# A hybrid attention and MoE block: the first norm without root instructions, its tiles turned one by one, key and value weights loaded first

## The chip, the cores and the metric

The kernel runs on one core of a Trainium2 chip. The metric is device time in microseconds (us) of one execution. The core's engines run side by side, each through a list of its own, and meet at semaphores: PE (TensorE, matrix products and transposes), DVE (VectorE), ACT (ScalarE), POOL (GpSimd), and SP (SyncE), which here only issues DMAs.

## The reference, cut to what matters

One decoder block over 512 tokens of width 1024, float32:

```
h = x * rsqrt(mean(x*x) + 1e-6) * g1              # first norm
q, kc, vc, ks, vs, kw, vw, gates, ... = split(h @ w_in)
x = x + mixed(attention of two kinds, from those) @ w_out
x = x + moe(rms_norm(x), 32 experts, top 4)       # 12 MB of weights per expert
out = rms_norm(x)
```

Rope turns the keys ks and kw and the query by cos and sin of position times frequency. The change touches the first line, the rope angles and the weights of the second line's first products.

## The kernel before

Tokens lie on the partitions in four tiles of 128 (NT = 4), the width in eight chunks of 128 (NK = 8). All order is written by hand: each engine's program is one list, with semaphore waits between.

The start, which the change touches, goes so. SP (L485 to L496) issues the four tiles of x (512 KB each), then g1 (1024 single numbers of 4 bytes), f_bias, the rope frequencies twice, the positions, then `w_small`: the 792 columns of w_in for kc, vc, ks, vs, kw, vw and the NSA gates (3168 KB), and 8 columns for the decay (32 KB), then weights of the compression, of the gates and of the query. ACT squares each tile with a sum per token (L917) and, once DVE has made mean + eps of the sum (L1692), takes the root of it (L919). DVE then inverts the root, refines it in four small instructions (L1685 to L1688), and multiplies the tile by it (L1694). PE turns the tiles by transposes against the identity (L1191): chunk after chunk, and within the chunk tile after tile, so that eight PSUM banks fill one after the other:

```
for c in range(NK):
    for t in range(NT):
        if c == 0: pe.wait_ge(x_normed, t + 1)
        last = pe.transpose(...)
    last.then_inc(full, 1)
```

DVE meanwhile works out the rope angles in 16 instructions over 128x512 (L1699 to L1708), and only then copies the odd chunks out of PSUM times g1 (L1716). ACT waits for these angles too, takes sin and cos (L922, L923), and then copies the even chunks (L929). PE waits for the whole of `w_small` and for all eight copies (L1193 to L1195), and then starts the products (L1181): kc, vc, ks, kw, vs, vw in seven banks and then the gates. A product is 8 chunks; in float32 each chunk shows as two matmul instructions.

After kc and vc, ACT copies them out (L935, L936), then ks and kw (L941). POOL multiplies these by the cos (L726), PE swaps their halves (L1227) and DVE adds the sin part. From L1284 on come attention, the mixing products, the second norm (whose inverse root POOL takes as a power, L806), the router, and the 32 experts, whose weights stream through a ring of 12 buffers as PE frees them. POOL's own list begins with constants: identity, mask, `swap`, cmp_neg, cmp_one, kT_cmp, v_cmp and ones8 (L695 to L722).

Of the kernel before, what the change touches and what calls it, by code (L numbers as in the profile page):

```python
# [15 lines left out]
P = 128  # L16
# [127 lines left out]
def hybrid_block(nc, x, positions, norm1_g, w_in, cmp_pos_emb, cmp_w1, cmp_w2, fox_f_bias, w_proj_nsa,  # L144
                 w_proj_fox, w_out, norm2_g, router_w, router_b, expert_w1, expert_b1, expert_w2,
                 expert_b2, norm_f_g, rope_freqs, out):
    with ExitStack() as ctx:
# [121 lines left out]
        small_loaded = sem("small_loaded")  # L269
        pos_loaded = sem("pos_loaded")  # L270
        w_small_loaded = sem("w_small_loaded")
        w_cmp_loaded = sem("w_cmp_loaded")
# [210 lines left out]
        def _(sp):  # L483
            for t in range(NT):
                sp.dma_start(xs[:, t, :], x_v[:, t, :]).then_inc(rows_loaded[t], 16)  # L485
            sp.dma_start(g1[:, :], norm1_g[0].rearrange("(c p) -> p c", p=P), allow_slow_non_contiguous=True).then_inc(small_loaded, 16)
            sp.dma_start(f_bias[:, :], fox_f_bias[0:1, :].partition_broadcast(P)).then_inc(small_loaded, 16)
            for g in range(G):
                sp.dma_start(freq[DH * g:DH * (g + 1), :], rope_freqs[:, :]).then_inc(pos_loaded, 16)
            sp.dma_start(pos_i, positions[0:1, :].partition_broadcast(P)).then_inc(pos_loaded, 16)  # L490
            sp.dma_start(w_small[:, :, 0:C_FQ - C_KC], w_in_v[:, :, C_KC:C_FQ]).then_inc(w_small_loaded, 16)
            sp.dma_start(w_small[:, :, C_FQ - C_KC:], w_in_v[:, :, C_FF:C_GN]).then_inc(w_small_loaded, 16)
            for j in range(2):
# [192 lines left out]
        def _(pool):  # L686
            step = Steps(pool, pool_step)

            def take(semaphore, value):
# [6 lines left out]
            pool.affine_select(out=ident[:, :], in_=ident[:, :], compare_op=ALU.not_equal, fill=1.0, base=0,  # L696
                               pattern=[[-1, P]], channel_multiplier=1).then_inc(consts, 1)
            step.link(pool.memset(mask[:, :], 0.0))
            tri = mask[:, S - P:S]
# [4 lines left out]
            for g in range(G):  # L704
                lo, hi = (swap[:, DH * g + half * k:DH * g + half * (k + 1)] for k in range(2))
                step.link(pool.affine_select(out=lo, in_=lo, compare_op=ALU.not_equal, fill=-1.0,
                                             base=-half - DH * g, pattern=[[-1, half]], channel_multiplier=1))
                ins = pool.affine_select(out=hi, in_=hi, compare_op=ALU.not_equal, fill=1.0,
                                         base=-DH * g, pattern=[[-1, half]], channel_multiplier=1)
                if g:  # L710
                    ins.then_inc(consts, 1)
                else:
                    step.link(ins)
            step.link(pool.memset(cmp_neg[:, :, :, :], 0.0))
            step.link(pool.memset(cmp_one[:, :, :, :], 1.0))
# [187 lines left out]
        def _(act):  # L903
# [11 lines left out]
            for t in range(NT):  # L915
                act.wait_ge(rows_loaded[t], 16)
                act.activation(xn[:, t, :], xs[:, t, :], ACT.Square, accum_out=ss1[:, t:t + 1]).then_inc(squares, 1)  # L917
                act.wait_ge(mean_sq, t + 1)
                act.activation(tmp1[:, t:t + 1], ss1[:, t:t + 1], ACT.Sqrt).then_inc(root, 1)  # L919

            act.wait_ge(angles, 1)
            act.activation(rope_sin[:, :], ang[:, 0, :], ACT.Sin).then_inc(sines, 1)  # L922
            act.activation(rope_cos[:, :], ang[:, 1, :], ACT.Sin).then_inc(sines, 1)  # L923
            pre = PreFills()
            act.wait_ge(small_loaded, 32)
            for c in range(0, NK, 2):
# [3 lines left out]
            for k, name in enumerate(("kc", "vc")):  # L930
                b, n = pre(name)
                act.wait_ge(work_full[b], n + 1)
                for g in range(G):
                    src = work(b)[g * DH:(g + 1) * DH, :]
                    act.activation(kv_c[0:DH, k, g, :], src, ACT.Copy).then_inc(act_step, 1)  # L935
                    last = act.activation(kv_c[DH:P, k, g, 0:S - 1], src[:, 1:S], ACT.Copy)  # L936
                last.then_inc(work_free[b], 1)
            for name, dst in (("ks", q_plain), ("kw", q_rope)):
                b, n = pre(name)
                act.wait_ge(work_full[b], n + 1)  # L940
                act.activation(dst, work(b), ACT.Copy).then_inc(work_free[b], 1)  # L941
                act.wait_ge(work_free[b], n + 1)
                act.sem_inc(raw_k_ready, 1)
# [227 lines left out]
        def _(pe):  # L1171
# [13 lines left out]
            pe.wait_ge(consts, 1)  # L1185
            for c in range(NK):
                w, full = bank(pre, "hT%d" % c)
                for t in range(NT):
                    if c == 0:
                        pe.wait_ge(x_normed, t + 1)  # L1190
                    last = pe.transpose(w[:, t * P:(t + 1) * P], xn[:, t, c * P:(c + 1) * P], ident[:, :])  # L1191
                last.then_inc(full, 1)
            pe.wait_ge(w_small_loaded, 32)  # L1193
            for b in range(NK):
                pe.wait_ge(work_free[b], 1)  # L1195

            def small(at, n):
                return lambda c: w_small[:, c, at - C_KC:at - C_KC + n]

            for name, at in (("kc", C_KC), ("vc", C_VC), ("ks", C_KS), ("kw", C_KW)):  # L1200
                w, full = bank(pre, name)
                matmuls(w, small(at, P), lambda c: hT[:, c, :], NK).then_inc(full, 1)
            for name, src, n, tiles in (("vs", small(C_VS, P), P, range(NT)), ("vw0", small(C_VW, N_VW), N_VW, (0, 1)),
# [464 lines left out]
        def _(dve):  # L1668
# [11 lines left out]
            def inverse_root(ss, r, t1, t2, count):  # L1680
# [7 lines left out]
                step.link(dve.tensor_tensor(r, r, t2, ALU.mult))  # L1688

            for t in range(NT):  # L1690
                dve.wait_ge(squares, t + 1)
                step.link(mean_square(ss1[:, t:t + 1], ss1[:, t:t + 1], EPS))  # L1692
                inverse_root(ss1[:, t:t + 1], rs1[:, t:t + 1], tmp1[:, t:t + 1], tmp2[:, t:t + 1], t + 1)
                dve.tensor_scalar(xn[:, t, :], xs[:, t, :], rs1[:, t:t + 1], None, ALU.mult).then_inc(x_normed, 1)  # L1694


            dve.wait_ge(pos_loaded, 48)
            turns_, a0, posf = ang[:, 2, :], ang[:, 3, :], ang[:, 3, :]
# [10 lines left out]
            dve.sem_inc(angles, 1)  # L1709

            dve.wait_ge(small_loaded, 32)
            pre = PreFills()
            for c in range(1, NK, 2):
                b, n = pre("hT%d" % c)
                dve.wait_ge(work_full[b], n + 1)
                dve.tensor_scalar(hT[:, c, :], work(b), g1[:, c:c + 1], None, ALU.mult).then_inc(work_free[b], 1)  # L1716


# [233 lines left out]
            def refined(t):  # L1952
                one = slice(t, t + 1)
                dve.wait_ge(power, t + 1)
                step.link(dve.scalar_tensor_tensor(tmp4[:, one], tmp3[:, one], ss2[:, one], tmp3[:, one], ALU.mult, ALU.mult))
# [239 lines left out]
            def finished(t):  # L2195
                dve.wait_ge(squares, 3 * NT + t + 1)
                step.link(mean_square(ss2[:, t:t + 1], ss2[:, t:t + 1], EPS))
                inverse_root(ss2[:, t:t + 1], rs2[:, t:t + 1], tmp3[:, t:t + 1], tmp4[:, t:t + 1], NT + t + 1)
                dve.scalar_tensor_tensor(y_in[t][:, 1, :], y_in[t][:, 0, :], rs2[:, t:t + 1], gf_b, ALU.mult, ALU.mult)\
                    .then_inc(result, 1)  # L2200

            dve.wait_ge(pos_loaded, 64)
            for t in range(NT):
# [24 lines left out]
```

## Time and profile before

| | us |
|---|---|
| median of 3 runs (lowest, highest) | 1676.53 (1675.32, 1678.14) |
| the profiled execution | 1675.77 |
| its span in the trace | 1674.0 |
| PE busy | 1591.8, 95% of the span |
| DVE, ACT, POOL busy | 440.9, 259.8, 233.9 |

The span runs from the first to the last instruction of the trace; 1.8 us of the execution's own time lie outside it. Busy shares are means over stages of different limits. Durations of PE's instructions are modelled, since they overlap in its pipeline: the distance between two starts is what one costs. Starts and durations are in us, "mean" and min/median/max of instructions in ns.

### The profile page before, as it was taken

Reading aid. Unit: us, or ns where it says so; the run is one execution under the profiler, and the core shown is the slowest. Engines: PE = TensorE matmul, PEld = TensorE weight load, DVE = VectorE, ACT = ScalarE, POOL = GpSimd, SP = SyncE. Lnnn points to the kernel's source line nnn. Section 1 sums busy time; section 2 is a strip of 40 time slices with the busy share of each in tenths; the row PEclk is TensorE's granted clock in tenths of the full one; section 3 lists DMA queues with packets and bytes.
Section 4 is the critical chain, followed back from the end, with each engine's and each line's share of the span. In section 5 each row is a group of like instructions: output and inputs, shape, how many; then the busy total and the mean of one; then the engine's idle time right before and its main releaser. Section 6 shows DMA issues by size and latency. Waiting matters only on the chain.

```text
span 1674.0 us, 32752 instructions
## 1 busy us (share of the span) xinstructions
PE 1591.8 (95%) x13380; PEld 645.9 (39%) x13381; DVE 440.9 (26%) x966; ACT 259.8 (16%) x541; POOL 233.9 (14%) x377
## 2 busy tenths in 40 slices
PE   5999999999999789999999999999999999999992
PEld 2654555565445323333333333333333333333331
DVE  4012555332325422113111311131112111211222
ACT  3212444323322100000000000000000000000002
POOL 1000000522200101111111111111111111121101
PEclk8999999999999799999999999999999999999996
DMA  8023120431251789999999999999999999999995
GB/s 224 1 54 73 38 76 13 136 88 51 65 200 51 275 342 376 388 393 386 396 386 395 392 399 386 391 394 399 389 396 399 401 389 394 400 402 390 400 383 177
DMA packets 150302, 472.35 MB, mean 282 GB/s; under 512 B 30537, under 2 KB 71497, under 8 KB 117458
## 3 DMA queue, kind: packets, MB, share of 16 engines
q1 hardware_dynamic: 137458, 446.56, 69.1%
q0 software_dynamic: 12800, 25.17, 6.9%
q8 instruction: 31, 0.51, 0.1%
q14 instruction: 13, 0.11, 0.0%
HBM read 452.41 MB, written 19.29 MB: 282 GB/s over the span
## 4 chain that ended last, share of the span: by engine, by line
PE 88%; DVE 5%; ACT 3%; issue 2%; DMA 1%; DVEq 0%; PEld 0%; POOL 0%; ACTq 0%; PEldq 0%; POOLq 0%; SPq 0%
PE ps L1562 40%; PE ps L1580 13%; PE ps L1181 12%; PE ps L1584 7%; PE ps L1510 3%; PE ps L1323 3%; PE ps L1308 2%; PE ps L1595 2%; PE ps L1536 2%; ACT mixT L995 2%; PE ps L1285 1%; ACT mixT L1004 1%; PE ps L1295 1%; DVE ps L1797 1%; PE ps L1556 1%
## 5 line engine op out<-in xcount | busy, mean ns | idle before, releaser
L1562 PE MATMUL ps<-ring,oT_fox 128*32 128x512 f32 x6144 | 668.8, 595 | 0.0
L1562 PEld LDWEIGHTS ps<-ring,oT_fox 128*32 128x32 f32 x6144 | 184.1, 110 | 462.8 <-issue 459.2
L1580 PE MATMUL ps<-ring,hT 128*32 128x512 f32 x2048 | 264.1, 592 | 0.0
L2101 DVE TENSOR_TENSOR mixT<-ps,mask 128x768 f32<-128x768 f32 x64 | 61.1, 954 | 650.2 <-PE ps L1562 650.2
L1584 PE MATMUL ps<-ring,hT 128*32 128x256 f32 x2048 | 154.8, 379 | 0.0
L1323 PE MATMUL ps<-hT,ring 128*128 128x512 f32 x304 | 137.3, 599 | 0.0
L1584 PEld LDWEIGHTS ps<-ring,hT 128*32 128x32 f32 x2048 | 61.3, 110 | 158.4 <-issue 158.4
L1119 ACT ACTIVATE mixT<-mixT 128x768 f32<-128x768 f32 x32 | 27.0, 845 | 609.8 <-DVE mixT L2105 609.8
L1181 PE MATMUL ps<-hT,ring 128*128 128x512 f32 x208 | 93.2, 609 | 7.0 <-ACT hT L929 7.0
L841 POOL COPY pT<-pT 96x32 bf16 (+1 forms) x64 | 13.8, 218 | 575.5 <-ACT hT L1129 566.3
L2130 DVE COPY hT<-ps 128x384 f32<-128x384 f32 x64 | 32.8, 553 | 181.0 <-PE ps L1595 180.9
L1323 PEld LDWEIGHTS ps<-hT,ring 128*128 128x128 f32 x304 | 55.5, 191 | 64.2 <-issue 64.2
L1129 ACT ACTIVATE hT<-ps,v_fox 128x512 f32<-128x512 f32 x64 | 33.7, 577 | 295.9 <-PE ps L1584 295.9
L1580 PEld LDWEIGHTS ps<-ring,hT 128*32 128x32 f32 x2048 | 61.1, 110 | 46.5
L1181 PEld LDWEIGHTS ps<-hT,ring 128*128 128x128 f32 x208 | 40.2, 195 | 56.5 <-issue 56.4
L995 ACT ACTIVATE mixT<-ps,st 128x128 f32<-128x128 f32 (+1 forms) x96 | 49.1, 536 | 78.1 <-DVE st L1803 78.1
L1510 PE MATMUL ps<-ring,mixT 128*128 128x512 f32 x128 | 59.0, 601 | 2.1 <-DVE qk L1930 2.1
L832 POOL DMA_INDIRECT x<-hT,v_win x32 | 50.6, 1580 | 26.2 <-POOL v_win L829 24.5
L834 POOL DMA_INDIRECT x<-hT,v_win x32 | 49.7, 1552 | 9.8 <-issue 9.8
L1181 PEld LDWEIGHTS ps<-ring,hT 128*128 128x128 f32 x384 | 45.2, 192 | 2.3 <-issue 2.3
L1181 PE MATMUL ps<-ring,hT 128*128 128x128 f32 (+1 forms) x384 | 45.5, 279 | 0.0
L818 POOL COPY v_win<-v_win 96x1 int32 (+1 forms) x30 | 5.9, 196 | 259.4 <-DMA x<-hT,v_win 231.0
(291 smaller groups left out, 1162.4 us busy)
## 6 DMA issues: line engine op xcount, KB each, us to landing
ring<-in_expert_w SPq DMA_DIRECT2D x384, 1024.0 KB, 19.8
ring<-in_w_in SPq DMA_DIRECT2D x28, 512.0 KB, 4.8
ring<-in_w_out SPq DMA_DIRECT2D x8, 512.0 KB, 7.6
ring<-in_w_in SPq DMA_DIRECT2D x1, 3168.0 KB, 12.9
xs<-in_x SPq DMA_DIRECT2D x4, 512.0 KB, 5.1
ring<-in_w_in SPq DMA_DIRECT2D x8, 256.0 KB, 3.6
ring<-in_w_proj_nsa SPq DMA_DIRECT2D x16, 128.0 KB, 2.9
ring<-in_w_proj_fox SPq DMA_DIRECT2D x8, 256.0 KB, 3.3
```

The source lines that it names most:

```text
L832: pool.indirect_dma_start(out=x2_half, out_offset=bass.IndirectOffsetOnAxis(ap=now_half[b], axis=0), in_=yb[b][:, 0:512], in_offset=None, ...
L834: pool.indirect_dma_start(out=x2_quarter, out_offset=bass.IndirectOffsetOnAxis(ap=now_quarter[b], axis=0), in_=yb[b][:, 512:768], in_offse ...
L995: last = act.activation(probs[:, h, P_OFF[t]:P_OFF[t] + P * (t + 1)], scores(h, t), ACT.Exp, bias=ngm[:, h, t:t + 1], accum_out=sums[:, h, ...
L1129: ins = act.activation(yb[b][:, cols], y_ps[:, cols], ACT.Copy, scale=gate)
L1181: last = pe.matmul(dst, lhs(c), rhs(c), start=(c == 0), stop=(c == n - 1))
L1308: ins = pe.matmul(o_bank[h * DH:(h + 1) * DH, kt * P:S], v[:, kt, h * DH:(h + 1) * DH], pT[:, h, at:at + S - kt * P], start=(first and n = ...
L1323: ins = pe.matmul(w, w_c(c), hT[:, c, :], start=(c == 0), stop=(c == NK - 1))
L1510: ins = pe.matmul(ps[:, u, :], mixT[:, k, t * P:(t + 1) * P], w_o[k][:, n * 512:(n + 1) * 512], start=(k == 0), stop=(k == NK - 1))
L1562: ins = pe.matmul(wide(ps[TG * j:TG * j + TG, g, :]), xT[b][:, c, TG * g:TG * g + TG], up_slab(c, j), start=(c == 0), stop=(c == NK - 1), ...
L1580: pe.matmul(ps[TG * q:TG * q + TG, 4, :], gT[b][:, 2 * (q // 2) + h, TG * j:TG * j + TG], ring[:, NK + j, at:at + 512], start=False, stop= ...
L1584: ins = pe.matmul(ps[TG * q:TG * q + TG, 5, 0:256], gT[b][:, 4 + h, TG * j:TG * j + TG], ring[:, NK + j, at:at + 256], start=False, stop=( ...
L2101: return dve.tensor_tensor(to, half, b_up[:, 256 * n:256 * n + 256].unsqueeze(1).broadcast_to([P, NG, 256]), ALU.add)
```

## The change

- ACT takes the four squares one after the other; its four roots go. POOL raises each mean to the power -0.5 (in between its constants, after `swap`), against a constant -0.5 that it writes into `hbias` first. DVE refines the power in three small instructions instead of a reciprocal and four, and makes the mean of the next tile before it refines this one.
- PE turns tile after tile, all eight chunks of a tile as soon as it is normed. The first product waits for each copied chunk as it comes to it, instead of for all eight ahead.
- DVE copies the odd chunks ahead of the angles. ACT copies the even chunks ahead of sin and cos, which it takes between its copies of kc and of vc.
- SP: the kc and vc columns (256 of the 792, 1024 KB) are loaded right behind x, ahead of g1, with a semaphore of their own. The other 536 columns (2144 KB) and the 8 of the decay come next, then f_bias, frequencies and positions, which come ahead of `w_small` in the kernel before.

```
@@ sync
             for t in range(NT):
                 sp.dma_start(xs[:, t, :], x_v[:, t, :]).then_inc(rows_loaded[t], 16)
+            sp.dma_start(w_small[:, :, 0:2 * P], w_in_v[:, :, C_KC:C_KC + 2 * P]).then_inc(w_kv_loaded, 16)
             sp.dma_start(g1[:, :], norm1_g[0].rearrange("(c p) -> p c", p=P), allow_slow_non_contiguous=True).then_inc(small_loaded, 16)
-            sp.dma_start(f_bias[:, :], fox_f_bias[0:1, :].partition_broadcast(P)).then_inc(small_loaded, 16)
+            sp.dma_start(w_small[:, :, 2 * P:C_FQ - C_KC], w_in_v[:, :, C_KC + 2 * P:C_FQ]).then_inc(w_small_loaded, 16)
+            sp.dma_start(w_small[:, :, C_FQ - C_KC:], w_in_v[:, :, C_FF:C_GN]).then_inc(w_small_loaded, 16)
+            sp.dma_start(f_bias[:, :], fox_f_bias[0:1, :].partition_broadcast(P)).then_inc(pos_loaded, 16)
             for g in range(G):
                 sp.dma_start(freq[DH * g:DH * (g + 1), :], rope_freqs[:, :]).then_inc(pos_loaded, 16)
             sp.dma_start(pos_i, positions[0:1, :].partition_broadcast(P)).then_inc(pos_loaded, 16)
-            sp.dma_start(w_small[:, :, 0:C_FQ - C_KC], w_in_v[:, :, C_KC:C_FQ]).then_inc(w_small_loaded, 16)
-            sp.dma_start(w_small[:, :, C_FQ - C_KC:], w_in_v[:, :, C_FF:C_GN]).then_inc(w_small_loaded, 16)
@@ gpsimd, after the identity; and after swap
+            step.link(pool.memset(hbias[:, :], -0.5))
...
+            for t in range(NT):
+                pool.wait_ge(mean_sq, t + 1)
+                pool.tensor_tensor(tmp1[:, t:t + 1], ss1[:, t:t + 1], hbias[:, :], ALU.pow).then_inc(power, 1)
@@ scalar
                 act.activation(xn[:, t, :], xs[:, t, :], ACT.Square, accum_out=ss1[:, t:t + 1]).then_inc(squares, 1)
-                act.wait_ge(mean_sq, t + 1)
-                act.activation(tmp1[:, t:t + 1], ss1[:, t:t + 1], ACT.Sqrt).then_inc(root, 1)
-            act.wait_ge(angles, 1)
-            act.activation(rope_sin[:, :], ang[:, 0, :], ACT.Sin).then_inc(sines, 1)
-            act.activation(rope_cos[:, :], ang[:, 1, :], ACT.Sin).then_inc(sines, 1)
...
                 last.then_inc(work_free[b], 1)
+                if k == 0:
+                    act.wait_ge(angles, 1)
+                    act.activation(rope_sin[:, :], ang[:, 0, :], ACT.Sin).then_inc(sines, 1)
+                    act.activation(rope_cos[:, :], ang[:, 1, :], ACT.Sin).then_inc(sines, 1)
@@ tensor
-            for c in range(NK):
-                w, full = bank(pre, "hT%d" % c)
-                for t in range(NT):
-                    if c == 0:
-                        pe.wait_ge(x_normed, t + 1)
+            for t in range(NT):
+                pe.wait_ge(x_normed, t + 1)
+                for c in range(NK):
+                    w, full = bank(pre, "hT%d" % c)
                     last = pe.transpose(w[:, t * P:(t + 1) * P], xn[:, t, c * P:(c + 1) * P], ident[:, :])
-                last.then_inc(full, 1)
-            pe.wait_ge(w_small_loaded, 32)
-            for b in range(NK):
-                pe.wait_ge(work_free[b], 1)
+                    if t == NT - 1:
+                        last.then_inc(full, 1)
+            def first_hT(c):
+                pe.wait_ge(work_free[c], 1)
+                return hT[:, c, :]
+            pe.wait_ge(w_kv_loaded, 16)
             for name, at in (("kc", C_KC), ("vc", C_VC), ("ks", C_KS), ("kw", C_KW)):
+                if name == "ks":
+                    pe.wait_ge(w_small_loaded, 32)
                 w, full = bank(pre, name)
-                matmuls(w, small(at, P), lambda c: hT[:, c, :], NK).then_inc(full, 1)
+                matmuls(w, small(at, P), first_hT if name == "kc" else lambda c: hT[:, c, :], NK).then_inc(full, 1)
@@ vector
+            first_mean(0)
             for t in range(NT):
-                dve.wait_ge(squares, t + 1)
-                step.link(mean_square(ss1[:, t:t + 1], ss1[:, t:t + 1], EPS))
-                inverse_root(ss1[:, t:t + 1], rs1[:, t:t + 1], tmp1[:, t:t + 1], tmp2[:, t:t + 1], t + 1)
-                dve.tensor_scalar(xn[:, t, :], xs[:, t, :], rs1[:, t:t + 1], None, ALU.mult).then_inc(x_normed, 1)
-            dve.wait_ge(pos_loaded, 48)
+                if t < NT - 1:
+                    first_mean(t + 1)
+                ss, r, t2, rs = (v[:, t:t + 1] for v in (ss1, tmp1, tmp2, rs1))
+                dve.wait_ge(power, t + 1)
+                step.link(dve.scalar_tensor_tensor(t2, r, ss, r, ALU.mult, ALU.mult))
+                step.link(dve.tensor_scalar(t2, t2, -0.5, 1.5, ALU.mult, ALU.add))
+                step.link(dve.tensor_tensor(rs, r, t2, ALU.mult))
+                dve.tensor_scalar(xn[:, t, :], xs[:, t, :], rs, None, ALU.mult).then_inc(x_normed, 1)
+            dve.wait_ge(small_loaded, 16)
+            (the four copies of the odd chunks, L1713 to L1716)
+            dve.wait_ge(pos_loaded, 64)
             (the angles, L1698 to L1709)
```

The counts of `power`, `root` and `pos_loaded` that later stages wait for are moved by the same numbers.

## Rows read from the trace of the kernel before

**Rows 1.** The page, first part: busy us, share of the span, instructions.
```profile
PE 1591.8 (95%) x13380; PEld 645.9 (39%) x13381; DVE 440.9 (26%) x966; ACT 259.8 (16%) x541; POOL 233.9 (14%) x377
```
**Rows 2.** What PE waited for, 0 to 150 us: total, times, longest.
```profile
PE ps L1191 <- DVE mixT L1694: 13.6, 4, 8.8
PE ps L1181 <- ACT hT L929: 7.0, 1, 7.0
```
**Rows 3.** The chain of waits, 0 to 150 us: start, length, what.
```profile
0.84 3.35 DMA xs<-in_x
...
23.45 0.44 DVE oT_nsa L1708
...
25.11 2.32 ACT hT L929 x4
27.78 60.12 PE ps L1181 x224
```
**Rows 4.** Windows: busy (x) of PE, PEld, DVE, ACT, POOL, granted clock, DMA share, GB/s.
```profile
27.80:33.00 5.20, 5.20 (x6) 2.13 (x7) 0.00 (x0) 0.00 (x0) 0.00 (x0) 0.50 1.08 252
33.00:34.00 1.00, 1.00 (x3) 0.53 (x2) 0.00 (x0) 0.00 (x0) 0.00 (x0) 0.74 1.35 218
...
548.00:576.00 28.00, 18.37 (x166) 10.76 (x168) 18.27 (x58) 4.35 (x7) 5.26 (x9) 0.63 0.77 270
```
**Rows 5.** Line L1181, the products, in 34:37 us.
```profile
L1181 PE MATMUL ps<-hT,ring x8: 592/592/593, 33.7 to 36.7; 128*128 128x512 f32 x8
```
**Rows 6.** Line L1191, the transposes, in 17:19 and 20.1:20.8 us: ns min/median/max, starts.
```profile
L1191 PE MATMUL ps<-ident,mixT x11: 421/421/421, 16.8 to 18.9; 128*128 128x128 f32 x11
...
L1191 PE MATMUL ps<-ident,mixT x6: 272/273/273, 19.9 to 20.5; 128*128 128x128 f32 x6
```
**Rows 7.** Timeline of PE, 10 to 180 us.
```profile
15.02 5.72 PE L1191 MATMUL ps<-ident,mixT 128*128 128x128 f32 x29 [1.64 <-DVE mixT L1694]
...
87.74 1.88 PE L1227 MATMUL ps<-qk,swap 128*128 128x512 f32 x4
```
**Rows 8.** Timeline of ACT, 0 to 30 us: start, length, instruction [idle before].
```profile
4.21 1.06 ACT L917 ACTIVATE mixT<-xs 128x1024 f32<-128x1024 f32 x1 [2.09 <-DMA xs<-in_x]
...
5.38 1.28 ACT L919 ACT_TABLE_LOAD   x1
```
**Rows 9.** Timeline of DVE, 0 to 30 us.
```profile
5.39 0.15 DVE L1678 TENSOR_SCALAR st<-st 128x1 f32<-128x1 f32 x1 [5.28 <-ACT mixT L917]
...
7.68 0.16 DVE L1688 TENSOR_TENSOR st<-st 128x1 f32<-128x1 f32 x1
7.88 0.75 DVE L1694 TENSOR_SCALAR mixT<-xs,st 128x1024 f32<-128x1024 f32 x1
...
14.88 0.42 DVE L1699 CAST oT_nsa<-oT_fox 128x512 f32<-128x512 int32 x1
...
24.10 2.73 DVE L1716 TENSOR_SCALAR hT<-ps,g 128x512 f32<-128x512 f32 x4 [0.23 <-DVE oT_nsa L1708]
```
**Rows 10.** Line L485 (loads of x): issue starts, then landing.
```profile
L485 SPq DMA_DIRECT2D xs<-in_x x4: 381/426/432, 0.8 to 2.2; - x4
...
DMA to landing us min/median/max: 3.3/5.1/6.9
```
**Rows 11.** Line L806, POOL's power in the second norm: ns min/median/max.
```profile
L806 POOL TENSOR_TENSOR v_win<-v_win,kT_win x4: 549/554/578, 496.5 to 550.9; 128x1 f32<-128x1 f32 x4
```
**Rows 12.** Timeline of SP's issues, 0 to 200 us.
```profile
2.69 0.47 SPq L486 DMA_DIRECT2D g<-in_norm_g  x1
...
7.24 3.08 SPq L492 DMA_DIRECT2D ring<-in_w_in  x1
```
**Rows 13.** DMA issues, 0 to 60 us: KB each, us from issue to landing.
```profile
ring<-in_w_in SPq DMA_DIRECT2D x1, 3168.0 KB, 12.9
...
ring<-in_w_in SPq DMA_DIRECT2D x1, 32.0 KB, 14.7
...
g<-in_norm_g SPq DMA_DIRECT2D x1, 4.0 KB, 5.9
```

More of the change, by code:

```diff
@@ L270, in hybrid_block @@
         pos_loaded = sem("pos_loaded")
+        w_kv_loaded = sem("w_kv_loaded")
         w_small_loaded = sem("w_small_loaded")
@@ L917, in _ @@
                 act.activation(xn[:, t, :], xs[:, t, :], ACT.Square, accum_out=ss1[:, t:t + 1]).then_inc(squares, 1)
-                act.wait_ge(mean_sq, t + 1)
-                act.activation(tmp1[:, t:t + 1], ss1[:, t:t + 1], ACT.Sqrt).then_inc(root, 1)
-            act.wait_ge(angles, 1)
-            act.activation(rope_sin[:, :], ang[:, 0, :], ACT.Sin).then_inc(sines, 1)
-            act.activation(rope_cos[:, :], ang[:, 1, :], ACT.Sin).then_inc(sines, 1)
             pre = PreFills()
-            act.wait_ge(small_loaded, 32)
+            act.wait_ge(small_loaded, 16)
             for c in range(0, NK, 2):
@@ L1688, in inverse_root, with first_mean @@
                 step.link(dve.tensor_tensor(r, r, t2, ALU.mult))
+            def first_mean(t):
+                dve.wait_ge(squares, t + 1)
+                mean_square(ss1[:, t:t + 1], ss1[:, t:t + 1], EPS).then_inc(mean_sq, 1)
+            first_mean(0)
             for t in range(NT):
-                dve.wait_ge(squares, t + 1)
-                step.link(mean_square(ss1[:, t:t + 1], ss1[:, t:t + 1], EPS))
-                inverse_root(ss1[:, t:t + 1], rs1[:, t:t + 1], tmp1[:, t:t + 1], tmp2[:, t:t + 1], t + 1)
-                dve.tensor_scalar(xn[:, t, :], xs[:, t, :], rs1[:, t:t + 1], None, ALU.mult).then_inc(x_normed, 1)
-            dve.wait_ge(pos_loaded, 48)
+                if t < NT - 1:
[7 more added lines that the diff above has]
+            dve.wait_ge(small_loaded, 16)
+            pre = PreFills()
+            for c in range(1, NK, 2):
+                b, n = pre("hT%d" % c)
+                dve.wait_ge(work_full[b], n + 1)
+                dve.tensor_scalar(hT[:, c, :], work(b), g1[:, c:c + 1], None, ALU.mult).then_inc(work_free[b], 1)
+            dve.wait_ge(pos_loaded, 64)
             turns_, a0, posf = ang[:, 2, :], ang[:, 3, :], ang[:, 3, :]
@@ L1709, in _ @@
             dve.sem_inc(angles, 1)
[L1711 to L1716, printed above, removed]
             for k in range(2):
@@ L1953, in refined @@
                 one = slice(t, t + 1)
-                dve.wait_ge(power, t + 1)
+                dve.wait_ge(power, NT + t + 1)
                 step.link(dve.scalar_tensor_tensor(tmp4[:, one], tmp3[:, one], ss2[:, one], tmp3[:, one], ALU.mult, ALU.mult))
@@ L2197, in finished @@
                 step.link(mean_square(ss2[:, t:t + 1], ss2[:, t:t + 1], EPS))
-                inverse_root(ss2[:, t:t + 1], rs2[:, t:t + 1], tmp3[:, t:t + 1], tmp4[:, t:t + 1], NT + t + 1)
+                inverse_root(ss2[:, t:t + 1], rs2[:, t:t + 1], tmp3[:, t:t + 1], tmp4[:, t:t + 1], t + 1)
                 dve.scalar_tensor_tensor(y_in[t][:, 1, :], y_in[t][:, 0, :], rs2[:, t:t + 1], gf_b, ALU.mult, ALU.mult)\
                     .then_inc(result, 1)
-            dve.wait_ge(pos_loaded, 64)
+            dve.wait_ge(pos_loaded, 80)
             for t in range(NT):
```

## The prediction, written before the changed kernel ran

> **What bounds the kernel now.** I read the busy shares first: PE works 95% of the span [rows 1], so only what keeps PE idle, or slow while busy, is to be had. Next, PE's waits in the first 150 us [rows 2]: 13.6 us for normed tiles and 7.0 us for copied chunks; these two are what it waits for ahead of the products. The chain of waits [rows 3] says what makes them: the load of x, the norm, then the rope angles on DVE (the last ends at 23.9), then ACT's even copies (25.11 + 2.32 = 27.4), and from 27.78 on PE without a break for 60 us. So the angles, which no product of that stretch needs, stand between the transposes and the products. What begins at 27.78 is the work of the whole kernel: each us by which it begins earlier is a us of the total, as long as no later wait is tied to something that does not move with it.
>
> The second thing to see is PE's pace. The products begin at half clock: 6 in 5.2 us at a granted 0.50, which is 1.2 GHz, and 0.74 in the next us, so the rise to 2.4 GHz came at about 33.5 [rows 4]. After it one costs (36.7 - 33.7) / 7 = 0.43 us [rows 5]. Half clock therefore cost (33.5 - 27.8) / 2 = 2.9 us. The transposes tell of the clock too: 10 starts in 16.8 to 18.9, so 0.21 each, and 421 ns of duration; later 272 ns and (20.5 - 19.9) / 5 = 0.12 each [rows 6]. So the clock rose there too, at about 19.9, some 4.9 us after PE's busy stretch began at 15.02 [rows 7].
>
> **The change part by part.** I rebuild the start in its new order, in trace time.
>
> *Squares.* The first square starts at 4.21 and DVE sees its sum at 5.39 [rows 8, 9], so a square holds ACT for about 1.2 us. The root, its table load of 1.28 and the wait for DVE's mean leave ACT's list [rows 8]. Then the loads count: x is issued at 0.8 to 2.2 and lands after 3.3 to 6.9 us, the last at 2.2 + 6.9 = 9.1 [rows 10]. The last square thus starts at about 9.4 (behind a third that lands in between) and its sum is there at 10.6; the third's at 9.4.
>
> *Power and refinement.* POOL's power is not in this place before; in the second norm it takes 0.55 [rows 11]. I take 0.65 with its semaphore, from 0.55 to 1.2 (twice). Before it, a mean is 0.2; behind it, three small instructions at 0.2 each and the multiplication of 0.75 [rows 9]: 1.35 of DVE for a tile. It makes the next mean ahead of that, so tile 0 ends at about 8.05 (5.39 + 0.2, second mean at 6.7, + 1.35), tile 1 waits for the third sum: 9.6 + 1.35 = 10.95; mean 3 at 11.15; tile 2 ends at 12.5, tile 3 at 13.85. The power runs beside this. The wait puts POOL's later constants (L714 to L722) behind the last power, at about 11.9; their first user on DVE comes after L1227 at 87.7 [rows 7]. Cost nothing; with the cover gone, each us of POOL would be one of PE.
>
> *Transposes.* 8 per tile: 8 x 0.213 = 1.7 us at half clock, 8 x 0.12 = 0.95 at full. At half: tile 0 in 8.2 to 9.9, tile 1 in 11.0 to 12.7, then without idle time 14.4 and 16.1. At full for the last tile alone 13.9 to 14.9. The first product needs these and the first copy: four on DVE take 2.73, so 0.7 each [rows 9], started when chunk 0 is full (13.95 to 14.6). Copies and transposes overlap; later chunks come every 0.35 us from two engines, and a chunk's two product instructions take 0.86: PE never waits for them. First product between 15.0 and 16.2; I take 15.8. Gain 27.8 - 15.8 = 12.0.
>
> *The clock.* Before, it rose 4.9 us after PE became busy in the transposes [rows 6, 7] and 5.7 after in the products [rows 4]. It was down again by the products because PE idled from 20.8 [rows 7] to 27.8. Now PE is busy from 11.0 with no such idle time behind. I take a rise at 16.3: a loss of 0.25 in place of 2.9, gain 2.6; between 0 (the loss stays 2.9) and 2.9.
>
> Here a page of the Trainium skill speaks against this term: "TensorE: Matmul & The Clock Gate", Part 4, PE-mode transpose, holds that transposes do not count as activity that brings the full clock. By this the products would start cold. The rows disagree, since transposes sped up from 421 to 272 ns with nothing but transposes running; I keep it as a rival.
>
> *Loads.* The kc and vc columns are 1024 KB behind 2048 KB of x. The old single load moved 3168 KB in 12.9 us [rows 13], 4.1 us per 1024 KB, so at worst they land 4.2 us behind x, at 13.3; with the rate of x itself (2048 KB by 9.1, from 0.84) at about 12. Either is before 15.8. g1 is issued about 0.5 later than at 2.69 [rows 12] and lands 5.9 after issue [rows 13]: 9.1, plus 2.6 to 4.2 for the 1024 KB now ahead of it: 11.7 to 13.3, against the 14 at which the first copy wants it. This has the smallest margin of all. If its 4-byte pieces mix with the 2144 KB behind them (8.7 us at that rate) it lands as late as 22. The other 2144 KB are wanted by ks, 32 products of 0.43 behind 15.8: 29.5. The decay columns, the last of the old order, landed at 7.24 + 14.7 = 21.9 [rows 12, 13] with the same bytes ahead. f_bias, frequencies and positions come behind them: by 24 at the latest. SP's issues of compression, gate and query weights keep their order and the bytes ahead of them.
>
> *Angles and sines.* 23.9 - 14.9 = 9.0 us of DVE, from 17 (copies done) or from 24: done at 26 to 33. ACT takes sin and cos between kc's and vc's copies, and holds vc, ks and kw behind them. PE first needs them for the swaps, at 87.7 [rows 7], which 14.6 earlier is 73.1: behind ACT's copies of vc, ks and kw and POOL's products with the cos there are 40 us of cover. Cost nothing; past it, 1 us for 1 us.
>
> *Sum.* 12.0 + 2.6 = 14.6 us. All later waits are for work or for buffers that move with PE, so I let it pass to the end. One thing can shift: the granted clock drops again in later pauses (0.63 in 548 to 576, [rows 4]), and where its rise falls within them can move by a us or two either way.
>
> Of the profiled execution, 1675.8 - 14.6 = 1661.2; the median of before lies 0.7 above that execution, so 1661.9 as a median. Two executions of before differ by up to 2.8 us, so about 0.2% (3.4 us) is what can be told from no change.
>
> **The rivals.**
> - *As summed.* 1661.9; its own range is 1658 (first product at 14.5 and full clock, 16.2 saved, and 2 for the later clock) to 1664. Chance 0.62.
> - *Transposes in pieces leave the clock down.* For: PE idles about 1.1 us between tiles 0 and 1. Against: [rows 6]. Products start at 16.2 and run 5.7 us at half: gain 11.6, time 1664.9 as a median. Chance 0.17. The page of the Trainium skill named above gives the same time.
> - *g1 or the kc and vc columns are late.* For: g1 is 1024 pieces of 4 bytes, now behind 1024 KB. First product at 19 to 22.5, the pause brings half clock back: gain 5.3 to 8.8, time 1667.5 to 1671. Chance 0.14.
> - *The gain is given back* (a weight load of the experts that does not move earlier, or the clock in a later pause): within 3.4 us of before, about 1675. Chance 0.03.
> - *Slower: the second load of `w_small` decides.* PE waits at ks for both the 2144 KB and the decay columns, which are 1024 pieces of 32 bytes. It costs 1 us for each us behind 29.5 at which they land, and makes the kernel slower only from 44 on; [rows 12, 13] have them at 21.9. At 50 the time would be 1682. Chance 0.03, with the same wait at ACT for angles past 60 in it.
> - *The change doesn't do what it says.* The copies and the products might still wait for all of `w_small`; the code shows none, and it would give 22, as in the case of g1. Chance 0.01.
>
> **How the numbers follow.** The likeliest is 1661.9. Low end 1657.5, the best of the first case less half the spread; high end 1669.5, into the late loads, with about 0.12 left above and 0.04 below. Faster by over 0.2%: 0.62 + 0.17 + 0.14 + 0.01 = 0.94; same 0.03; slower 0.03.
>
> **What would show it.** The chain from x to the first product with L1181 at 14.5 to 16.2; no angle in that chain; PE's wait for copies near nothing; transposes in four groups; products at 0.43 from the start or within 1 us; POOL's first power near 5.6 and 0.55 long; sin and cos between 26 and 33. Wrong: a first product past 18, a half-clock stretch of over 3 us in the products, PE waiting before ks, or a distance between first product and end that has grown by over 3 us.

## The result, and the profile after

| | before | after |
|---|---|---|
| median, us | 1676.6 | 1661.1 |
| lowest to highest | 1675.3 to 1678.1 | 1660.4 to 1661.4 |
| profiled execution (span) | 1675.8 (1674.0) | 1660.9 (1659.2) |

The ratio is 0.9906, with a 95% interval of 0.9895 to 0.9918: 15.5 us, faster, clear of the noise. The forecast was 1661.9, in a range of 1657.5 to 1669.5. Measured twice more (e1, e11 below), the same changed kernel took 1660.9 and 1661.9 us beside 1676.8 and 1675.9 for before.

What PE waited for in the first 150 us of the changed kernel (engine, line, releaser: total us, times, longest), to be held against [rows 2]:

```profile
PE ps L1195 <- DVE mixT L1713: 8.5, 2, 8.3
...
PE ps L1186 <- ACT hT L930: 0.2, 1, 0.2
```

The wait for the copied chunks was 7.0 us and is 0.2. Of the 8.5 us for normed tiles 8.3 are the wait ahead of the first tile. The chain of waits over the same stretch (start, length, what), against [rows 3]:

```profile
1.75 5.57 DMA xs<-in_x
7.33 1.16 ACT mixT L923 x2
...
12.00 0.88 DVE mixT L1713
12.93 0.34 PE ps L1195
13.36 0.70 ACT hT L930
14.19 57.28 PE ps L1186 x224
...
93.17 15.63 PE ps L1186 x32
```

No angle is left in it. The first product starts at 14.19 where it started at 27.78, and the 224 instructions that follow take 57.28 us where they took 60.12: that is 13.6 and 2.8 us, together 16.4 us ahead. The last row is read further down.

DVE and POOL, from their timelines, against [rows 9, 11]. DVE makes the first mean at 5.44, as before (5.39); the fourth tile's multiplication starts at 12.00 in place of 14.21:

```profile
5.44 0.15 DVE L1688 TENSOR_SCALAR st<-st 128x1 f32<-128x1 f32 x1 [5.32 <-ACT mixT L923]
...
12.00 0.87 DVE L1713 TENSOR_SCALAR mixT<-xs,st 128x1024 f32<-128x1024 f32 x1
13.49 2.72 DVE L1720 TENSOR_SCALAR hT<-ps,g 128x512 f32<-128x512 f32 x4 [0.61 <-PE ps L1195]
20.23 0.43 DVE L1724 CAST oT_nsa<-oT_fox 128x512 f32<-128x512 int32 x1 [4.02 <-DMA oT_fox<-in_positions]
```

```profile
5.67 0.58 POOL L719 TENSOR_TENSOR st<-st,hbias 128x1 f32<-128x1 f32 x1 [1.52 <-DVE st L1688]
...
10.98 0.74 POOL L721 MEMSET cmp_one<- 128x256 f32 x1
```

The angles start when the positions land, at 20.2; sin follows at 29.3. The loads (KB each, us from issue to landing), against [rows 13]:

```profile
ring<-in_w_in SPq DMA_DIRECT2D x1, 2144.0 KB, 12.9
...
ring<-in_w_in SPq DMA_DIRECT2D x1, 1024.0 KB, 8.6
...
g<-in_norm_g SPq DMA_DIRECT2D x1, 4.0 KB, 8.5
```

Issued at 2.69, 3.24 and 4.36, these three landed at 11.3 (kc and vc columns), 11.7 (g1) and 17.3 (the rest). The first copy starts at 13.36, on ACT, so g1 had 1.6 us to spare.

The clock. Transposes (line L1195) in 9.4:11 and in 11:12.5 us, and the first products (L1186) in 14:17, ns min/median/max, then starts:

```profile
L1195 PE MATMUL ps<-ident,mixT x8: 421/421/468, 9.4 to 10.9; 128*128 128x128 f32 x8
L1195 PE MATMUL ps<-ident,mixT x13: 272/273/421, 10.7 to 12.5; 128*128 128x128 f32 x13
```

```profile
L1186 PE MATMUL ps<-hT,ring x7: 593/593/667, 14.2 to 16.8; 128*128 128x512 f32 x7
```

As in [rows 6], 421 ns is a transpose at half clock and 272 one at full; their distances, 0.21 and 0.11 us, halve as well. The short ones begin at 11.7, and the first clock record of the trace, full, stands at 11.65. So the rise came there, while PE had run nothing but transposes, and every product, from the first, ran at full clock. In e1 and e11 the same rise came at 13.3 and 13.6. The windows can't show it, since they count the time ahead of the first record as full clock. Here is 8 to 11 us, with transposes of 421 ns (busy of PE, PEld, DVE, ACT, POOL, then clock, DMA share, GB/s):

```profile
8.00:11.00 3.00, 2.70 (x13) 2.54 (x14) 2.43 (x11) 1.63 (x4) 1.38 (x4) 1.00 1.13 332
```

### The profile page after: what moved, and what is told of

It reads as the page before. It is cut to its first block, busy times and chain, and to the rows that moved or that the text cites. A ratio compares the mean times of both kernels' runs of the same rounds, so it can differ in the third digit from the quotient of the medians.

```text
span 1659.2 us, 32738 instructions
## 1 busy us (share of the span) xinstructions
PE 1589.3 (96%) x13380; PEld 645.0 (39%) x13381; DVE 438.8 (26%) x958; ACT 258.1 (16%) x536; POOL 237.3 (14%) x382
## 4 chain that ended last, share of the span: by engine, by line
PE 89%; DVE 4%; ACT 3%; issue 2%; DMA 1%; DVEq 0%; PEld 0%; POOL 0%; SPq 0%; ACTq 0%; PEldq 0%; POOLq 0%
PE ps L1572 40%; PE ps L1590 13%; PE ps L1186 12%; PE ps L1594 7%; PE ps L1520 4%; PE ps L1333 3%; PE ps L1318 2%; ACT mixT L1000 2%; PE ps L1605 2%; PE ps L1546 2%; PE ps L1295 1%; ACT mixT L1009 1%; PE ps L1305 1%; PE ps L1566 1%; DVE ps L1814 1%
## 5 line engine op out<-in xcount | busy, mean ns | idle before, releaser
L847 POOL COPY pT<-pT 96x32 bf16 (+1 forms) x64 | 13.7, 216 | 574.6 <-ACT hT L1134 565.4
L1186 PE MATMUL ps<-hT,ring 128*128 128x512 f32 x208 | 92.1, 603 | 0.2 <-ACT hT L930 0.2
L1186 PEld LDWEIGHTS ps<-hT,ring 128*128 128x128 f32 x208 | 39.7, 193 | 49.0 <-issue 48.8
L1186 PEld LDWEIGHTS ps<-ring,hT 128*128 128x128 f32 x384 | 45.2, 192 | 2.3 <-issue 2.3
L1186 PE MATMUL ps<-ring,hT 128*128 128x128 f32 (+1 forms) x384 | 45.5, 279 | 0.0
## 6 DMA issues: line engine op xcount, KB each, us to landing
ring<-in_w_in SPq DMA_DIRECT2D x1, 2144.0 KB, 12.9
```

The costliest lines, as they stand in the source:

```text
L1186: last = pe.matmul(dst, lhs(c), rhs(c), start=(c == 0), stop=(c == n - 1))
```

## The experiments

All times are medians. e1 to e4, e5 to e8, e9 to e11, and e12 are four groups, each measured beside its own runs of the kernel before, whose medians were 1676.8, 1676.3, 1675.9 and 1677.2; the ratios are to these. "Rest" is the time from the swaps after ks and kw (L1227 before) to the end of the span: what lies behind the stretch that the change touches. Starts are in us of each run's one trace.

| | median, us | ratio to before (95%) | first product | swaps | rest |
|---|---|---|---|---|---|
| before | 1676.6 | | 27.8 | 87.7 | 1586.3 |
| changed | 1661.1 | 0.9906 (0.9895, 0.9918) | 14.2 | 71.3 | 1587.9 |
| e1 again | 1660.9 | 0.9905 (0.989, 0.992) | 14.8 | 71.9 | 1587.5 |
| e2 old loads | 1669.6 | 0.9956 (0.9941, 0.9971) | 20.8 | 79.5 | 1588.2 |
| e3 angles first | 1679.6 | 1.0016 (1.0007, 1.0026) | 31.2 | 91.3 | 1586.3 |
| e4 split | 1661.9 | 0.9911 (0.9897, 0.9924) | 15.1 | 72.2 | 1587.3 |
| e5 roots back | 1664.1 | 0.9921 (0.9907, 0.9935) | 16.7 | 73.8 | 1588.8 |
| e6 by chunk | 1664.1 | 0.9932 (0.9919, 0.9946) | 18.5 | 75.5 | 1586.8 |
| e7 all copies | 1664.4 | 0.9925 (0.9912, 0.9939) | 17.8 | 76.6 | 1587.4 |
| e8 copies only | 1669.2 | 0.9951 (0.9938, 0.9965) | 21.2 | 78.3 | 1590.2 |
| e9 last norm | 1664.4 | 0.9934 (0.992, 0.9947) | 15.6 | 72.7 | 1590.0 |
| e10 third on ACT | 1665.1 | 0.9938 (0.9925, 0.9952) | 14.5 | 71.6 | 1592.1 |
| e11 again | 1661.9 | 0.9922 (0.9908, 0.9935) | 15.0 | 72.2 | 1588.0 |
| e12 third only | 1662.1 | 0.9909 (0.9892, 0.9925) | 14.0 | 71.2 | 1587.6 |

### e1 and e11: the changed kernel again

No edit.

> The changed kernel itself, once more. In its trace the first product starts 13.6 us earlier and all products run at full clock (another 2.9), so PE is 16.4 us ahead at the swaps (87.9 against 71.5); but the span is only 14.8 shorter. 1.7 is lost at 93 to 97, right behind the small products of the compression, where the granted clock is 0.50, and 1.7 more at 464 to 468; before has neither of these dips. Theory: the time of the start is fixed, and the dips are not part of the change: they fall in or out with where PE's thin stretches lie in time, so a second execution shows the first product within 0.3 us of 14.2, and either dip may be missing (a span 1.7 shorter) or there. Rival: the dips are made by the new schedule and stand in every execution at the same places; then this trace shows both, and the median is 1661.1 again with a spread under 1 us.

> The changed kernel a third time, beside e9 and e10. Theory (half-clock stretches fall in and out, the start is fixed up to the landing of x): first product at 14.2 to 15.2, the time from the swaps to the end 1587 to 1588, median 1661 within 1. Rival: a trace with both dips again at 93 and 464, as in the first.

The chain of e1 (start, length, what), and granted clock in windows of the first trace of the changed kernel (busy of PE, PEld, DVE, ACT, POOL, then clock, DMA share, GB/s):

```profile
14.82 57.28 PE ps L1186 x224
...
93.84 13.93 PE ps L1186 x32
```

```profile
92.00:96.00 4.00, 4.00 (x37) 2.37 (x35) 1.51 (x8) 0.26 (x1) 0.00 (x0) 0.70 0.07 15
96.00:100.00 4.00, 4.00 (x9) 1.67 (x8) 0.00 (x0) 0.00 (x0) 0.00 (x0) 0.88 0.00 0
```

In the first trace the 32 products behind the compression took 15.63 us, 1.7 more than the 13.93 in e1 and e11: a half-clock stretch lies at 93.6 to 97.0, and e1 and e11 have none there. The stretch at 466 is in the first and in e11 (464), missing in e1, and e1 has one at 286 to 290 that the first has not. The theory holds as far as that they come and go between executions of one program while the median stays; what makes one fall in is not shown. The first product came at 14.2, 14.8 and 15.0: e1's 0.3 bound was too tight, since the last of x lands at 8.5 to 9.1 and the clock rose at 11.7, 13.3 and 13.6, within the transposes.

### e2: the old loads

```
-            sp.dma_start(w_small[:, :, 0:2 * P], w_in_v[:, :, C_KC:C_KC + 2 * P]).then_inc(w_kv_loaded, 16)
...
             sp.dma_start(pos_i, positions[0:1, :].partition_broadcast(P)).then_inc(pos_loaded, 16)
+            sp.dma_start(w_small[:, :, 0:C_FQ - C_KC], w_in_v[:, :, C_KC:C_FQ]).then_inc(w_small_loaded, 16)
+            sp.dma_start(w_small[:, :, C_FQ - C_KC:], w_in_v[:, :, C_FF:C_GN]).then_inc(w_small_loaded, 16)
...
-            pe.wait_ge(w_kv_loaded, 16)
+            pe.wait_ge(w_small_loaded, 32)
```

> The changed kernel with the loads of the kernel before: x, g1, f_bias, frequencies, positions, the 792 columns in one piece, the 8 decay columns; the first product waits for all of them. Theory (the split load is what lets products start at 14.2): they landed at 21.9 before, so the first product starts at about 22, 7.8 later, after a pause of PE of 8 us, and begins at half clock for some 5 us (2.9 lost): 10 to 11 us slower than the changed kernel, about 1671.5. Rival (the columns are there anyway, the order of the loads buys little because x and g1 are what is waited for): under 3 us slower, below 1664.

The chain:

```profile
7.54 13.25 DMA ring<-in_w_in
20.84 58.84 PE ps L1184 x224
```

The first product starts at 20.8, released by the decay columns, after a pause of PE of 5.8 us. The products take 58.84 instead of 57.28, so 1.6 us are lost to half clock. The median is 8.7 us above e1's (the traces' starts give 6.0 and 1.6): the theory, under its 10 to 11, since the columns landed 1.1 us earlier than it had them, e1 itself started 0.6 later than the first trace that the sum was made from, and half clock cost 1.6 and not 2.9.

### e3: the angles first again

On DVE the 16 instructions of the angles stand ahead of the four copies again, and on ACT:

```
+            act.wait_ge(angles, 1)
+            act.activation(rope_sin[:, :], ang[:, 0, :], ACT.Sin).then_inc(sines, 1)
+            act.activation(rope_cos[:, :], ang[:, 1, :], ACT.Sin).then_inc(sines, 1)
             pre = PreFills()
             act.wait_ge(small_loaded, 16)
```

> The changed kernel with the rope angles on DVE and sin and cos on ACT ahead of the copies again, all else as changed, the positions behind the weights in the load order too. Theory: the angles cannot start before the positions land (20.2 in the changed kernel's trace), take 9 us, and then come sin, cos and the copies: first product at 31 to 33, half clock for over 5 us: 17 to 19 + 2.9 = 20 to 22 us slower than the changed kernel, 1681 to 1683, so slower than the kernel before. Rival (the angles are short of the weights anyway, so their place is worth only what lies behind 22): first product near 27, about 1677.

The chain:

```profile
15.47 4.78 DMA oT_fox<-in_positions
...
29.89 0.61 ACT rope_cos L927
30.51 0.58 ACT hT L933
31.23 60.24 PE ps L1185 x224
```

As the theory had it: first product at 31.2, at half clock, 18.7 us above e1, and a kernel that is no faster than before, and by its interval 0.07% to 0.26% slower, though norm, loads and transposes are all changed. The new load order puts the positions at 20.2, and is good only together with the new place of the angles.

### e5, e6, e7: one part undone each

In e5 ACT's roots, DVE's reciprocal and its four instructions are back and POOL's powers gone:

```
+                act.wait_ge(mean_sq, t + 1)
+                act.activation(tmp1[:, t:t + 1], ss1[:, t:t + 1], ACT.Sqrt).then_inc(root, 1)
```

In e6 the two loops of the transposes are exchanged again, in e7 the single wait is back:

```
-            for t in range(NT):
-                pe.wait_ge(x_normed, t + 1)
-                for c in range(NK):
+            for c in range(NK):
+                for t in range(NT):
```

```
+            for b in range(NK):
+                pe.wait_ge(work_free[b], 1)
```

> The changed kernel with ACT's roots and DVE's reciprocal and four refinement instructions again in the first norm; POOL's powers gone. Theory (the roots held ACT's next square and set the pace of a tile to 2.1 us, as in the kernel before): the last tile is normed near 15.0 instead of 12.9, the first product starts at 16.2 to 16.5 instead of 14.2 to 14.8 in the two traces of the changed kernel: 1.5 to 2.2 us slower. Rival (x lands at 8.6 only and sets the pace, so the roots were hidden): under 0.7 us.

> The changed kernel with transposes chunk by chunk again, so that 29 of 32 wait for the last normed tile at 12.9. Theory (PE and its clock): 29 transposes, first at 0.21 us and the last few at 0.12 as in the kernel before, end at about 18.5; first product at 18.6 to 19, at full clock; 4 to 5 us slower. Rival (the copies are what the first product waits for, and turning early is worth only the 1.7 us by which 8 transposes at half clock exceed 1): under 2.5 us.

> The changed kernel with one wait for all eight copied chunks ahead of the first product. Theory: the last copy ends at 16.2, so the first product starts at 16.3 instead of 14.2; the pause of 2.4 us leaves the clock full: 1.7 to 2.3 us slower. Rival (the pause brings half clock back): 2.9 more, 5 us slower.

The first product's row of the chain in e5, e6 and e7, then e7's wait and its clock (same columns as above):

```profile
16.68 57.28 PE ps L1184 x224
```

```profile
18.62 57.04 PE ps L1186 x224
```

```profile
17.82 58.97 PE ps L1186 x224
```

```profile
PE ps L1186 <- DVE hT L1718: 2.4, 1, 2.4
```

```profile
17.80:24.00 6.20, 6.18 (x11) 2.70 (x12) 3.44 (x7) 0.00 (x0) 0.00 (x0) 0.72 0.86 164
```

e5: the first product starts 1.6 to 2.5 us later than in the three traces of the changed kernel; from the last landing of x on it is 1.2 to 1.9 later. That is the theory, in its trace. e6: 3.4 to 4.3 later (its first product starts at 18.46, just before the last transpose ends), at full clock; a little under the theory. In e7 the first product starts at 17.8 in place of the foretold 16.3, since the last of x landed at 9.1 and the clock rose only at 14.8, so that the transposes ended later. And a second point was foretold wrong: behind the pause of 2.4 us the clock fell, at 18.2, and the products took 1.7 us more. This is its one trace, of an execution of 1665.8 us; the others took 1662.3 to 1666.6, and whether each of them had the fallen clock is not shown.

The medians say less. No changed kernel was measured in this group; against before the three gain 12.2, 12.3 and 11.9 us, the changed kernel 15.9, 14.0 and 15.5 in its groups. So each part is worth about 2 to 4 us, and the interval of each ratio overlaps with that of e11.

### e8: the copies alone, on the kernel before

DVE's four copies stand ahead of its angles, and on ACT:

```
-            act.wait_ge(angles, 1)
-            act.activation(rope_sin[:, :], ang[:, 0, :], ACT.Sin).then_inc(sines, 1)
-            act.activation(rope_cos[:, :], ang[:, 1, :], ACT.Sin).then_inc(sines, 1)
...
+                if k == 0:
+                    act.wait_ge(angles, 1)
...
```

> The kernel before with one part of the change alone: the copies ahead of the angles on DVE, and ahead of sin and cos on ACT, which takes these between kc and vc. Loads, roots, transposes and the two waits of the first product as before. Theory: transposes end at 20.8, the decay columns land at 21.9, the copies end by 22.3, so the first product starts near 22.3 in place of 27.8, after a pause of PE of 1.5 us only, at full clock: gain 5.5 + 2.9 = 8.4 us over the kernel before, about 1668.3. Rival (clock not kept): the first product starts at 22.3 at half clock, gain 5.5, 1671.2.

PE's wait and the chain:

```profile
PE ps L1182 <- DMA ring<-in_w_in: 1.0, 1, 1.0
```

```profile
21.16 57.28 PE ps L1182 x224
```

A pause of 1.0 us left the clock full: theory. The median is 7.2 us below before's, not the 8.4 foretold: at the swaps the trace is 9.4 us ahead, and its rest is 3.9 longer than before's, with half-clock stretches at 100 and 472 that before has not, beside one at 141 that stands for before's at 150, and a longer one from 544 on.

This one reordering of two engines' lists is about half of the whole gain; the load order is the other half only once it is there. A comparison with e2 shows the same for the rest: e2 has the roots, the tile-wise transposes and the wait chunk by chunk as well, but the old loads, and its first product starts at 20.8 against 21.2 here. Its transposes end at 15.0 in place of 20.1, and PE then waits 5.8 us for the columns and loses its full clock. Without the new load order these three parts bring nothing: 1669.6 against 1669.2, or 7.1 and 7.2 us of gain over before.

### e4: full products between the thin ones

```
+            pe.wait_ge(w_gate_loaded[0], 64)
+            project_gate(pre, "gn2", 0, 0)
             for l in range(CB // 2):
                 for k in range(2):
                     last = pe.matmul(w[DH * k:DH * (k + 1), n:n + 1], w_c1[:, k, l, :], pos_c[:, k, l:l + 1],
...
-            project_gates(2)
+            project_gate(pre, "gf2", 0, 1)
```

> The changed kernel with one of the two gate products of the third gate pair (gn2, 6.9 us of full products) moved between the two loops of small products of the compression (64 of 62 columns, 64 of one column, 5.6 us together). Theory: the clock fell at 93 because these 5.6 us use little of the array; with full products between them no half-clock stretch follows, and the median is 1.0 to 1.7 us lower, 1659.4 to 1660, if the dip stands in most executions of the changed kernel. Rival (the dip is chance, or comes from elsewhere): within 0.5 us of the changed kernel, or a half-clock stretch is still seen at 90 to 105.

The chain of e4:

```profile
88.27 3.61 PE ps L1254 x60
91.89 7.06 PE ps L1186 x16
98.95 1.96 PE ps L1260 x64
100.91 0.34 PE ps L1266 x4
101.25 8.76 PE ps L1186 x16
```

The half-clock stretch is there all the same, behind the second loop (8.76 us against 7.06), and the median is 1.0 us above the changed kernel's. My remedy failed. Of the 14 traces here, six have a stretch behind the compression (changed, e2, e4, e8, e10, e12). That thin products cause it is not shown, only that it stands behind them when it comes.

### e9: the last norm treated alike

```
-                act.wait_ge(mean_sq, 2 * NT + t + 1)
-                act.activation(tmp3[:, t:t + 1], ss2[:, t:t + 1], ACT.Sqrt).then_inc(root, 1)
+                pool.wait_ge(mean_sq, 2 * NT + t + 1)
+                pool.tensor_tensor(tmp3[:, t:t + 1], ss2[:, t:t + 1], minus_half, ALU.pow).then_inc(power, 1)
```

> The changed kernel with the same treatment of the last norm, which ends the program: no roots on ACT, POOL's power of each mean against its constant -0.5, three refinement instructions on DVE, the next mean ahead of the multiplication. Theory (this norm is on the path to the end, one tile's DVE work after the other): in the kernel before a tile takes 2.65 us (starts of its last DVE instruction 1661.76, 1664.40, 1667.05, 1669.69) and the first is ready for it 2.4 after its mean, with a table load of 1.28 in that. With powers a tile takes 2.05 (0.15 + 0.6 + 1.29) and the first 1.5: 0.9 + 3 x 0.6 = 2.7 us faster than the changed kernel, 1658.3. Rival (the loads of the rows and the stores behind set this end): under 0.8 us.

POOL at the end of e9, and DVE's first two tiles:

```profile
1649.64 0.57 POOL L909 TENSOR_TENSOR v_win<-v_win,kT_win 128x1 f32<-128x1 f32 x1 [13.72 <-issue]
1651.12 1.51 POOL L909 TENSOR_TENSOR v_win<-v_win,kT_win 128x1 f32<-128x1 f32 x1 [0.91 <-DVE v_win L1689]
```

```profile
1644.14 0.15 DVE L1689 TENSOR_SCALAR v_win<-v_win 128x1 f32<-128x1 f32 x1 [24.89 <-ACT ring L1174]
...
1650.24 0.22 DVE L2222 SCALAR_TENSOR_TENSOR v_win<-v_win 128x1 f32<-128x1 f32 x1 [5.95 <-POOL v_win L909]
...
1652.67 0.22 DVE L2222 SCALAR_TENSOR_TENSOR v_win<-v_win 128x1 f32<-128x1 f32 x1 [0.44 <-POOL v_win L909]
```

2.5 us slower than e11 beside it, where 2.7 faster was expected. The mean is there at 1644.3, but POOL takes it up at 1649.6. The 13.7 us ahead of that are no rest: POOL's list waits until 1639.4 for its last scatter to land, and from 1640.2 to 1649.5 it goes through the loop over extra expert blocks, 21 times with nothing to do, 0.44 us each. Its sequencer's rows show the loop:

```profile
L889 POOLq ALU_OP  x21: 32/32/38, 1640.6 to 1649.4; - x21
```

In the kernel before and in the changed one nothing comes behind this loop on POOL, so its length does not matter there. And a power that meets DVE's multiplication takes 1.51 in place of 0.57. A tile takes 2.43 in place of 2.65, which wins back 0.7. From the first mean to the end of the span e9 takes 18.6 us, the changed kernel 14.7.

### e10 and e12: the third tile multiplied by ACT

```
+            act.activation(xn[:, 2, :], xs[:, 2, :], ACT.Copy, scale=rs1[:, 2:3]).then_inc(third_normed, 1)
```

> e9 with, in the first norm, the multiplication of the third tile on ACT instead of DVE, so that DVE refines the fourth meanwhile. Theory: the fourth tile is normed 0.7 us earlier and the first product starts that much earlier, if x lands as before: 0.5 to 0.7 us faster than e9, which only its trace can tell (the distance from the last landing of x to the first product: 14.19 - 8.6 = 5.6 in the changed kernel, 5.0 here). Rival (turning the third tile is what holds the fourth): the distance stays 5.6.

> The changed kernel with the third tile of the first norm multiplied on ACT, the last norm as before. In e10 the last tile of x landed at 9.2 and the first product started at 14.5, 5.3 later; in four traces with DVE alone it took 5.6 to 6.3 (5.6 in the changed kernel, 6.3 in e1, 5.9 in e11, 6.3 in e9). Theory: 5.0 to 5.4 here, so the median is 0.5 to 1 us under the changed kernel's 1661.1: 1660.3. Rival (the clock's half stretches, 1.7 us each, cover a gain of this size): a median anywhere in 1659.5 to 1662.5, not told from the changed kernel.

e10 is on e9, e12 on the changed kernel. From the last landing of x to the first product: 5.3 and 5.5 us, against 5.6, 6.3, 5.9 in the changed kernel's three traces and 6.3 in e9. But the distance hangs on the clock too, which rose in the transposes at 11.7, 13.3 and 13.6 in the changed kernel's traces, at 15.1 in e9, 12.2 in e10 and 11.8 in e12. e12 and the first trace, alike in this, differ by nothing (5.54 against 5.57). And in e12 PE waits for a normed tile once only, ahead of the first:

```profile
PE ps L1202 <- DVE mixT L1724: 8.7, 1, 8.7
```

From 8.7 on it turns tiles without a break, so what holds the first product is the turning, as e10's rival had it. An earlier fourth tile can be worth little: PE waits 0.2 us for it in the first trace and not at all in e1 and e11. The medians (1665.1 beside 1664.4; 1662.1) show no gain either. No version measured here beats the changed kernel.

## Why the prediction was right

The total was met within 0.8 us, but with some luck: the start gained 1.8 us more than summed, and 1.6 us of the lead were lost behind it, which the sum did not have.

- *What bounds.* Right: the angles ahead of the copies and the loads behind them held the products. e3 shows the one (18.7 us above e1), e2 the other (8.7).
- *First product at 15.8, gain 12.0.* It came at 14.2, gain 13.6, just outside the 14.5 to 16.2 that I gave as the sign; at 14.8 and 15.0 in e1 and e11. The tiles were ready at 12.9 in place of 13.85, since the third of x landed at 7.3 and the last at 8.6, not 9.1; and from 11.7 on the transposes ran at full clock. The sign "transposes in four groups" did not come: tiles 0 to 2 are turned in one go, with one short wait ahead of tile 3.
- *The clock, 2.6.* It was 2.8: [rows 3] have 60.12 for the 224 instructions, after has 57.28. The clock came up with nothing but transposes running, at 11.7 in place of 16.3; at 13.3 and 13.6 in e1 and e11, still ahead of the products. "TensorE: Matmul & The Clock Gate" in the Trainium skill (Part 4, PE-mode transpose) says that the full clock does not engage for them. The rows above decide against it for the float32 transposes of this kernel, and the rival that it stood beside, 1664.9, fell.
- *Power, POOL's constants, sines: nothing.* Right. A power took 0.55 to 0.58 us in the first norm. POOL's constants ended at 14.1, sin and cos came at 29.3 to 30.4, and PE came to the swaps without a wait.
- *g1 late.* It landed at 11.7, the early end of my 11.7 to 13.3. The kc and vc columns landed at 11.3, 2.7 behind x. My "about 12" for them did not follow from the rate that I gave for it, which is the same 4.1 us per 1024 KB as the other; it is the spacing of x's landings (1.3 to 1.8 us per 512 KB) that holds here.
- *All of it passes to the end.* Not quite: 16.4 us ahead at the swaps, 14.8 in the span. The difference of 1.6 is a balance of half-clock stretches. The first trace has short ones at 94, 135 and 466, before's has one at 150, each worth about 1.7 us, so those at 135 and 150 cancel; [rows 4] show a later one that both have, and it is 20.5 us long in before, 17.1 here. Matched instruction by instruction, the lead is 14.8 us behind the first stretch (DVE's copy at 123.89 and 109.08), 13.2 behind the third (486.35 and 473.17), 14.1 behind the later one (591.59 and 577.48) and 14.8 at the last norm (1659.36 and 1644.57). The stretch at 94 also lies in products and is over the 3 us that I named as a sign of being wrong; in the first 224 products, which that term was about, there is none. e1 and e11 show the stretches moving between executions. With one trace of before I can't say whether before has fewer of them in the mean: over the medians of three groups the gain is 15.5, 15.9 and 14.0, where the swaps of their traces give 15.6 to 16.4.

Taken apart, roots and powers, tile-wise transposes and the wait chunk by chunk are worth about 2 to 4 us each, the loads 8.7, and the copies alone 7.2 on the kernel before. Their sum means nothing: each undone part also moves what the next one waits for, and its clock, and the first three are worth nothing with the old loads (e2 against e8).

## What to carry to other kernels

Look on the chain of waits for work that the next stage does not need (here 9 us of angles), and move it behind what that stage waits for; then look again, because a load or a clock is what waits next, and a reordering that pays in one state of the other parts costs in another (e3). Count PE's pauses along with its work: the pause of 1.0 us cost its length alone, those of 2.4, 5.8 and 7.0 us (e7, e2, before) cost 1.7, 1.6 and 2.8 us more, in half clock behind them. Before work is given to an idle engine, look where its list is at that time: what the busy share calls idle was, in e9, 3.5 us of waiting for a DMA and 9.3 us of an empty loop.

## What the runs showed of the hardware

- Between executions of one program, the places of half-clock stretches move: 94, 135, 466 in one; 133, 286 in the next; 133, 464 in a third. The one at 94 cost 1.7 us, with PE busy all through (4.00 of 4 us in 92 to 96, at a granted 0.70).
- A pause of PE of 2.4 us was followed by half clock (e7), one of 1.0 us was not (e8). Each is one trace, and half clock also came with no pause at all.
- POOL and DVE slow each other. POOL's memset of 128x256 took 0.74 beside DVE's multiplication from SBUF to SBUF and 0.31 alone, that multiplication 0.89 in place of 0.75, and the power of one column 1.51 in place of 0.57 beside a DVE instruction of 1.28. "SBUF — State Buffer" in the Trainium skill (SBUF: two separate sides) describes a port pair that POOL and certain DVE instructions take in turns for a whole instruction. These rows agree with it, but for one: a first memset, started 0.04 us after the same multiplication, took its 0.31.
- The clock rises within transposes: 421 to 272 ns, at 19.9 in before and at 11.7 in the changed kernel, at 13.3 and 13.6 in its other two traces.
- Going through a loop with nothing to do takes time on POOL's sequencer, none of it counted as busy: 21 rounds of 0.44 us in e9.
